# A hybrid decoder layer on one core: a recurrent head's last level computed from copies of its operands, right behind the level ahead of it

## The chip, the cores and the metric

The kernel runs on one core of a Trainium2 chip. It is written by hand for each engine: TensorE (PE) does matrix products into eight PSUM banks, VectorE (DVE) and ScalarE (ACT) do the elementwise work, GpSimd (POOL) sets up constants and SyncE (SP) issues the DMAs. The engines run side by side and meet only at semaphores that one raises and another waits for. The metric is the device time of one execution in microseconds (us), the median of several runs.

## What is computed

One decoder layer over 512 tokens of width 1024. A conditioned RMSNorm, one input projection, two groups of four heads each (a gated linear recurrence, HGRN2, and top-k sparse attention), one output projection, and a gated feed-forward part. The change touches the recurrent group only:

```python
def step(S, inp):
    qb, kb, vb, gb = inp            # gb: cumulated log of the forget gate f
    o_inter = einsum('bhtk,bhkv->bhtv', qb * exp(gb), S)
    diff = gb[:, :, :, None, :] - gb[:, :, None, :, :]
    decay = exp(where(causal[None, None, :, :, None], diff, -inf))
    A = einsum('bhtk,bhsk,bhtsk->bhts', qb, kb, decay)
    o_intra = einsum('bhts,bhsv->bhtv', A, vb)
    g_last = gb[:, :, -1]
    S_new = exp(g_last)[..., None] * S + einsum('bhsk,bhsv->bhkv', kb * exp(g_last - gb), vb)
    return S_new, o_inter + o_intra
```

So an output token t takes from each earlier token s the value v_s with weight q_t · k_s, and every channel of that product is shrunk by the product of the gates f between s and t.

## The kernel before

**Levels.** The kernel doesn't run the recurrence in time. For each head it builds the whole 512 x 512 triangle of weights in 10 levels (`LEVELS`, numbered 0 to 9). Level 0 is the diagonal. Level st from 1 pairs neighbouring blocks of `half` = 2^(st-1) tokens: keys of the left block with queries of the right one. The arrays `k_b` (keys) and `q_f` (queries), both 128 channels x 512 tokens, carry the product of gates inside their block. After each level st from 1 to 8, DVE widens the blocks in place: right halves of `q_f` times the total of the left block (L1105), left halves of `k_b` times the total of the right block (L1107), and the totals themselves pairwise (L1110, into `tot`). Since this is in place, DVE waits for PE's matmuls of the level (`lvl_mm`) first, and PE's next level waits for DVE (`lvl_ready`). Level 8 has two products of 128 x 128 (L1598), level 9 two of 128 x 256 (L1602): key blocks 0 and 1 against query blocks 2 and 3 together. Levels alternate between PSUM banks 2 and 3, which ACT (outer levels: L607, L608, L619, L624, L625, L627) and DVE (inner levels) empty.

**Filling.** Between two levels PE computes steps of the input projection of the next head, of four weight tiles f, q, i and g with 8 steps each. A step is three matmuls of 128 x 512 (L1342): the operands are split into a high and a low part. `LEVEL_STEPS` says how many of the 32 steps follow each level (31 of them; the last stands behind the output product of the head, L1629). In the last recurrent head the steps are those of the first attention head, 24 in place of 32, in the same proportion. Then follow one step, the sum of squares (L1637) and the next head.

**DVE's other work.** In the same levels DVE runs the top-k search of the attention (`LEVEL_ROUNDS`: 12 rounds for each head, a MAX8 at L1075 and a MATCH_REPLACE8 at L1080 each, over 256, 384 or 512 columns), and the low parts of weights (`split_lo`, L817). In the text of a level the order is: wait for `lvl_mm`, widen, MAX8s of its rounds, copy of an inner level, MATCH_REPLACE8s, `split_lo`. Rounds 7 and 8 stand in level 7, round 9 in level 8, rounds 10 and 11 in level 9. After level 9 come `hp` and `f_w` (L1083 to L1091), the start of the next head, or, after the last head, `att_rotate` (L1149 to L1154), for which PE waits at L1646. Heads 0 and 3 are written out for DVE, heads 1 and 2 are a loop; for PE heads 0 to 2 are a loop.

Of the kernel before, what the change touches and what calls it, by code (L numbers as in the profile page):

```python
# [30 lines left out]
P = 128  # L31
D_MODEL = 1024
SEQ = 512
# [24 lines left out]
IDX_COLS = IDX_HEADS * IDX_DIM + IK_COLS  # L58
IDX_ORDER = (4, 0, 1, 2, 3)
LEVELS = 10  # L60
LEVEL_STEPS = (0, 5, 3, 5, 2, 4, 4, 3, 3, 2)
LEVEL_ROUNDS = ((0,), (), (1, 2), (), (3, 4), (5,), (6,), (7, 8), (9,), (10, 11))
PARTNER_HEAD = [(r + 16) % 32 for r in range(32)]
ROUNDS = TOPK // 8
# [8 lines left out]
def build(nc, x, c, positions, w_ada, b_ada, norm_pre_mix, norm_post_mix, norm_pre_ffn, norm_post_ffn, w_in,  # L73
          hgrn_lower_bound, hgrn_out_norm, idx_k_norm_w, idx_k_norm_b, w_out, w_ffn_in, w_ffn_out, rope_const, out):
    f32, f32r, u32, i32 = mybir.dt.float32, mybir.dt.float32r, mybir.dt.uint32, mybir.dt.int32
    ALU, ACT = mybir.AluOpType, mybir.ActivationFunctionType
    ds = bass.ds
    ctx = ExitStack()
    with ctx:
# [12 lines left out]
        act = sb("act", FT * SEQ)  # L92
# [31 lines left out]
        def part(t, at, n=SEQ):  # L124
            return t[:, at:at + n]

        f_, q_silu = part(act, 0), part(act, 2 * SEQ)
        q_f, k_b, tot, i_t, i_tok, o_sq, o_rstd, o_n = (part(act, n * SEQ) for n in range(5, 13))
        att_hg = act[:, 13 * SEQ:13 * SEQ + 2560]  # L130
        at_diag = att_hg.rearrange("p (c x) -> p c x", x=SEQ + P)[:, :, 0:P]
# [72 lines left out]
        lvl_ready, lvl_mm, lvl_out, tot_ok = sem("lvl_ready"), sem("lvl_mm"), sem("lvl_out"), sem("tot_ok")  # L204
# [600 lines left out]
        def _(ve):  # L805
            V = nc.vector
# [7 lines left out]
            def split_lo(g, slot, n=1024):  # L814

                ve.wait_ge(hi_ok, g + 1)
                V.tensor_tensor(w_lo[slot][:, 0:n], w_raw[slot][:, 0:n], w_hi[slot][:, 0:n].bitcast(f32),  # L817
                                ALU.subtract).then_inc(lo_ok, 1)
# [250 lines left out]
            def hg_body(h):  # L1069
                def find_eight(n):  # L1070

                    t = n % 3 + 1
                    if not (isinstance(h, int) and h == 0 and n < 3):
                        wait_apart(top_rep, h * 12 + (n - 2))
                    V.max(top8[:, 8 * (t - 1):8 * t], sc_t[t]).then_inc(top_max, 1)  # L1075

                def take_eight(n):
                    t = n % 3 + 1
                    wait_apart(top_max, h * 12 + (n + 1))
                    V.match_replace(out=sc_t[t], in_to_replace=top8[:, 8 * (t - 1):8 * t], in_values=sc_t[t],  # L1080
                                    imm_value=TAKEN).then_inc(top_rep, 1)

                V.tensor_copy(hp[:, :], hg_par[:, ds(h * 3, 2)]).then_inc(hp_ok, 1)  # L1083
                ve.wait_ge(f_sig, h + 1)
                ve.wait_ge(hp_ok, 1 if isinstance(h, int) and h == 0 else h * 2)
                V.tensor_scalar(f_w, f_, hp[:, 0:1], hp[:, 1:2], ALU.mult, ALU.add).then_inc(f_ok, 1)
                ve.wait_ge(f_ok, h + 1)
                V.tensor_scalar(k_b, f_w, float(-HEAD ** -0.5), float(HEAD ** -0.5), ALU.mult,
                                ALU.add).then_inc(lvl_ready, 1)
                ve.wait_ge(q_ok, h + 1)  # L1090
                V.tensor_tensor(q_f, q_silu, f_w, ALU.mult).then_inc(lvl_ready, 1)  # L1091
                t_off = 0
                src = f_w
                for st in range(LEVELS):
                    half = 0 if st == 0 else 1 << (st - 1)
                    ve.wait_ge(lvl_mm, h * LEVELS + (st + 1))
                    if 0 < st < LEVELS - 1:

                        nb = SEQ // (2 * half)
                        qv = q_f.rearrange("p (b two h) -> p b two h", two=2, h=half)  # L1100
                        kv = k_b.rearrange("p (b two h) -> p b two h", two=2, h=half)
                        tv = src.rearrange("p (b two) -> p b two", two=2)
                        if st > 1:
                            ve.wait_ge(tot_ok, h * 8 + (st - 1))
                        V.tensor_tensor(qv[:, :, 1, :], qv[:, :, 1, :],  # L1105
                                        tv[:, :, 0:1].to_broadcast([P, nb, half]), ALU.mult)
                        V.tensor_tensor(kv[:, :, 0, :], kv[:, :, 0, :],  # L1107
                                        tv[:, :, 1:2].to_broadcast([P, nb, half]), ALU.mult).then_inc(lvl_ready, 1)
                        nxt = tot[:, t_off:t_off + nb]
                        V.tensor_tensor(nxt, tv[:, :, 0], tv[:, :, 1], ALU.mult).then_inc(tot_ok, 1)  # L1110
                        src, t_off = nxt, t_off + nb
                    rounds = LEVEL_ROUNDS[st]
                    for n in rounds:
                        find_eight(n)

                    pv = ps[2 + st % 2][:, 0:P].rearrange("p (c t) -> p c t", c=TT)
                    bv = blk.rearrange("p (c t) -> p c t", c=TT)
                    m = block_masks[:, None, min(st, 5) * 32:(min(st, 5) + 1) * 32]
                    if st == 0:
                        if not (isinstance(h, int) and h == 0):  # L1120
                            ve.wait_ge(blk_out, h)
                        V.tensor_tensor(bv, pv, m.to_broadcast([P, TT, 32]), ALU.mult).then_inc(lvl_out, 1)
                    elif st < 6:
                        wait_apart(lvl_out, h * 6 + st)
                        V.copy_predicated(bv, m.bitcast(u32).to_broadcast([P, TT, 32]), pv).then_inc(lvl_out, 1)
                    if st == 1:
                        if not (isinstance(h, int) and h == 0):
                            head_tail(h - 1)
                    for n in rounds:
                        take_eight(n)  # L1130
                    if isinstance(h, int) and h == HG_HEADS - 1:
                        if st in (1, 4, 9):
                            split_lo(*{1: (G_ATT + 1, 1), 4: (G_ATT + 2, 2), 9: (G_ATT + 3, 0)}[st])
                    elif st in (1, 3, 6, 8):
                        at, slot = {1: (5, 1), 3: (6, 2), 6: (7, 3), 8: (8, 0)}[st]
                        split_lo(h * 4 + (G_HG + at), slot)

            hg_body(0)
            with ve.Fori(1, HG_HEADS - 1) as h:
# [193 lines left out]
        def _(te):  # L1333
            mm = nc.tensor.matmul
# [83 lines left out]
            for t in range(TT):  # L1418
# [3 lines left out]
                for half in range(2):  # L1422
                    if t == 3 and half:
                        te.wait_ge(xt_high, 1)
                    for k in range(4):
                        at = t * D_MODEL + (4 * half + k) * P
                        last = nc.tensor.transpose(ps[2 * (t % 3) + half][:, k * P:(k + 1) * P], xn[:, at:at + P],
                                                   ident[:, :])
# [144 lines left out]
            def hg_body(h, last_head):  # L1573
                def level(st):
                    te.wait_ge(lvl_ready, h * LEVELS + (st + 1))
                    if st == 0:
                        te.wait_ge(q_ok, h + 1)

                    if 2 <= st < 8:
                        te.wait_ge(lvl_out, h * 6 + (st - 1))  # L1580
                    elif st >= 8:
                        te.wait_ge(outer_out, h * 4 + (st - 7))
                    bank = ps[2 + st % 2]
                    q = q_f if st else q_silu
                    if st < 7:
                        ahead = 32 if st == 6 else 0
                        for t in range(TT):
                            for j in (0, 2) if st == 6 else range(4):
                                at = t * P + 32 * j
                                last = mm(bank[32 * j:32 * j + 32, t * 32:(t + 1) * 32], k_b[:, at:at + 32],  # L1590
                                          q[:, at + ahead:at + ahead + 32], start=True, stop=True)
                    elif st == 7:
                        for t in range(TT):
                            last = mm(bank[0:64, t * 64:(t + 1) * 64], k_b[:, t * P:t * P + 64],
                                      q_f[:, t * P + 64:(t + 1) * P], start=True, stop=True)
                    elif st == 8:
                        for b in range(2):
                            last = mm(bank[:, b * P:(b + 1) * P], k_b[:, 2 * b * P:(2 * b + 1) * P],  # L1598
                                      q_f[:, (2 * b + 1) * P:(2 * b + 2) * P], start=True, stop=True)
                    else:  # L1600
                        for b in range(2):
                            last = mm(bank[:, b * 2 * P:(b + 1) * 2 * P], k_b[:, b * P:(b + 1) * P],  # L1602
                                      q_f[:, 2 * P:4 * P], start=True, stop=True)
                    last.then_inc(lvl_mm, 1)

                def project(n, count):
# [9 lines left out]
                for t in range(TT):  # L1616
                    last = nc.tensor.transpose(ps[6][:, t * P:(t + 1) * P], i_t[:, t * P:(t + 1) * P], ident[:, :])
# [91 lines left out]
            h = ATT_HEADS - 1  # L1709
# [142 lines left out]
```

## Time and profile before

| | us |
|---|---|
| median of 3 runs | 726.9 (726.54 to 729.52) |
| the profiled execution | 728.42 |
| its span in the trace | 726.7 |
| PE busy | 705.7 (97% of the span) |
| DVE busy | 434.0 (60%) |
| ACT busy | 296.2 (41%) |
| heads 0 to 3 of the recurrence, from 103.9 to 227.0 | 123.1 |

The profiled execution took 1.5 us more than the median, and 1.7 us of it lie outside the span of the instructions. A row of a timeline gives the start of an instruction and its length. The length of a matmul goes up to a modelled end, and the next one starts before that: what a matmul costs is read from the distance between starts. A floating-point matmul appears as two passes, so the two products of level 8 are a row of `x4`.

### The profile page before, as it was taken

The numbers are of one execution on the slowest core, as the hardware profiler recorded it, in microseconds if no ns is written. First come the engines' busy times: TensorE is split into PE (matmuls) and PEld (weight loads), VectorE is DVE, ScalarE is ACT, GpSimd is POOL, SyncE is SP. The second block draws the span as 40 slices with busy tenths as digits, with TensorE's granted clock in tenths as the row PEclk, the third lists the DMA queues.
The fourth block names the chain that finished last, engine by engine and source line by source line (L and its number), as shares of the span: only waits on it lengthen the run. The fifth ranks groups of instructions, "written<-read, shape, count | busy, mean of one in ns | idle before, by whom it ended". The sixth has DMA issues, their size and how long they took to land.

```text
span 726.7 us, 11020 instructions
## 1 busy us (share of the span) xinstructions
PE 705.7 (97%) x3962; PEld 552.7 (76%) x3962; DVE 434.0 (60%) x806; ACT 296.2 (41%) x472; POOL 11.1 (2%) x39
## 2 busy tenths in 40 slices
PE   5999999999999999999999999999999999999997
PEld 4565567777766878878888888888888788888885
DVE  3966678898898999968643433323432335443444
ACT  6445553535454444536572343342343332211223
POOL 4000000000000000000000000000000000000000
PEclk9999999999999999999899999999999999999999
DMA  9944023231222766567225532355533224223202
GB/s 314 358 144 114 3 59 85 62 116 53 62 60 87 217 217 223 182 209 205 81 59 145 144 105 78 106 144 144 144 94 108 87 87 132 99 87 102 71 0 117
DMA packets 95995, 89.10 MB, mean 123 GB/s; under 512 B 2950, under 2 KB 84954, under 8 KB 95964
## 3 DMA queue, kind: packets, MB, share of 16 engines
q1 hardware_dynamic: 95964, 88.70, 39.9%
q8 instruction: 18, 0.29, 0.2%
q14 instruction: 13, 0.11, 0.0%
HBM read 86.59 MB, written 2.10 MB: 122 GB/s over the span
## 4 chain that ended last, share of the span: by engine, by line
PE 61%; DVE 4%; issue 1%; ACT 0%; DVEq 0%; ACTq 0%
PE ps L1342 34%; PE ps L1363 17%; PE ps L1381 6%; DVE rope L892 1%; PE ps L1646 1%; PE ps L1402 1%; PE ps L1529 1%; DVE w_lo L817 1%; PE ps L1666 1%; PE ps L1778 1%; PE ps L1782 1%; PE ps L1779 1%; PE ps L1523 0%; DVE act L1149 0%; DVE res L1154 0%
## 5 line engine op out<-in xcount | busy, mean ns | idle before, releaser
L1342 PE MATMUL ps<-h_hi,w_hi 128*128 128x512 f32 x560 | 227.3, 406 | 0.0
L1342 PE MATMUL ps<-h_hi,w_lo 128*128 128x512 f32 x560 | 218.7, 391 | 0.0
L1342 PE MATMUL ps<-h_lo,w_hi 128*128 128x512 f32 x560 | 218.3, 390 | 0.0
L817 DVE TENSOR_TENSOR w_lo<-w_raw,w_hi 128x1024 fp32r<-128x1024 f32 (+1 forms) x109 | 129.3, 1187 | 99.4 <-ACT w_hi L462 98.9
L462 ACT ACTIVATE w_hi<-w_raw 128x1024 fp32r<-128x1024 f32 (+1 forms) x109 | 111.6, 1029 | 105.9 <-PE ps L1363 86.3
L1342 PEld LDWEIGHTS ps<-h_hi,w_hi 128*128 128x128 f32 x560 | 105.2, 188 | 30.3 <-issue 9.1
L1342 PEld LDWEIGHTS ps<-h_hi,w_lo 128*128 128x128 f32 x560 | 105.1, 188 | 22.6
L1342 PEld LDWEIGHTS ps<-h_lo,w_hi 128*128 128x128 f32 x560 | 105.3, 188 | 20.7 <-issue 1.0
L1363 PE MATMUL ps<-w_hi,h_hi 128*128 128x512 f32 x176 | 70.1, 398 | 0.8 <-DVE mix L1214 0.8
L1363 PE MATMUL ps<-w_hi,h_lo 128*128 128x512 f32 x176 | 68.6, 390 | 0.0
L1363 PE MATMUL ps<-w_lo,h_hi 128*128 128x512 f32 x176 | 68.5, 389 | 0.0
L794 ACT ACTIVATE adaw<-ps 128x512 f32<-128x512 f32 x22 | 13.2, 598 | 132.0 <-PE ps L1342 130.2
L1272 DVE TENSOR_TENSOR act<-adaw,ps 128x512 f32 (+1 forms) x22 | 15.1, 687 | 57.2 <-PE ps L1342 57.2
L1295 DVE CAST h_hi<-act 128x512 fp32r (+1 forms) x22 | 9.4, 426 | 56.8 <-PE ps L1363 53.7
L1363 PEld LDWEIGHTS ps<-w_hi,h_hi 128*128 128x128 f32 x176 | 33.0, 188 | 8.3 <-DVE mix L1214 1.0
L1363 PEld LDWEIGHTS ps<-w_lo,h_hi 128*128 128x128 f32 x176 | 33.1, 188 | 7.2 <-issue 0.5
L1363 PEld LDWEIGHTS ps<-w_hi,h_lo 128*128 128x128 f32 x176 | 33.0, 188 | 6.9
L1075 DVE MAX8 top<-score 128x8 f32<-128x256 f32 (+2 forms) x48 | 25.2, 552 | 6.1 <-PE ps L1590 5.8
L1080 DVE MATCH_REPLACE8 score<-top,score 128x256 f32<-128x256 f32 (+2 forms) x48 | 25.8, 543 | 0.0
L1381 PE MATMUL ps<-w_hi,h_hi 128*128 128x512 f32 x64 | 24.9, 389 | 0.0
L1381 PE MATMUL ps<-w_lo,h_hi 128*128 128x512 f32 x64 | 24.9, 389 | 0.0
L1381 PE MATMUL ps<-w_hi,h_lo 128*128 128x512 f32 x64 | 24.9, 389 | 0.0
(250 smaller groups left out, 791.9 us busy)
## 6 DMA issues: line engine op xcount, KB each, us to landing
w_raw<-in_w_ffn_in SPq DMA_DIRECT2D x44, 512.0 KB, 5.7
w_raw<-in_w_in SPq DMA_DIRECT2D x28, 512.0 KB, 3.8
w_raw<-in_w_ffn_out SPq DMA_DIRECT2D x22, 512.0 KB, 3.5
adaw<-in_w_ada SPq DMA_DIRECT2D x12, 512.0 KB, 3.9
act<-in_w_ada SPq DMA_DIRECT2D x12, 512.0 KB, 9.2
adaw<-in_w_ada SPq DMA_DIRECT2D x6, 1024.0 KB, 5.3
act<-in_w_ada SPq DMA_DIRECT2D x6, 1024.0 KB, 5.1
res<-in_x SPq DMA_DIRECT2D x8, 512.0 KB, 4.7
```

Of the source, the lines that this page charges most:

```text
L462: sc.activation(w_hi[slot][:, 0:n], w_raw[slot][:, 0:n], ACT.Copy).then_inc(hi_ok, 1)
L794: sc.activation(silu_g[u // 2], ps[u][:, :], ACT.Silu).then_inc(silu_done[u // 2], 1)
L817: V.tensor_tensor(w_lo[slot][:, 0:n], w_raw[slot][:, 0:n], w_hi[slot][:, 0:n].bitcast(f32), ALU.subtract).then_inc(lo_ok, 1)
L892: V.scalar_tensor_tensor(out=total, in0=w, scalar=silu, in1=total, op0=ALU.mult, op1=ALU.add).then_inc(sum_used, 1)
L1075: V.max(top8[:, 8 * (t - 1):8 * t], sc_t[t]).then_inc(top_max, 1)
L1080: V.match_replace(out=sc_t[t], in_to_replace=top8[:, 8 * (t - 1):8 * t], in_values=sc_t[t], imm_value=TAKEN).then_inc(top_rep, 1)
L1272: V.tensor_tensor(act[:, ds(i * 2 * SEQ + v * SEQ, SEQ)], silu_g[v], ps[2 * v + 1][:, :], ALU.mult).then_inc(act_ok[v], 1)
L1295: V.tensor_copy(h_hi[:, at], act[:, ds(k * SEQ, SEQ)]).then_inc(xs_hi, 1)
L1342: last = mm(ps[bank][0:rows, :], a, b, start=(k == 0 and n == 0), stop=(k == KT - 1 and n == 2))
L1363: last = mm(ps[2 * t + b][:, :], a, w, start=(first and n == 0), stop=(last_one and n == 2))
L1381: last = mm(ps[2 * t + b][:, :], a, w, start=False, stop=(n == 3 and m == 2))
L1402: return nc.tensor.transpose(ps[k][:, t * P:(t + 1) * P], xn[:, t * D_MODEL + k * P:t * D_MODEL + (k + 1) * P], ident[:, :])
```

## The change

1. `LEVEL_STEPS` goes from `..., 4, 4, 3, 3, 2` to `..., 4, 4, 4, 0, 4` for levels 5 to 9: four steps ahead of level 8, none between levels 8 and 9, four behind.
2. `q_last` and `k_last`, 128 columns each, are new places in a part of `act` that nothing else uses at that time.
3. In level 8 DVE no longer widens in place. It writes `q_last` from query block 3 and `k_last` from key block 0, with no wait for PE's level 8; the third operation, the totals, is left out. `tot_ok` so counts 7 for each head.
4. In level 9 DVE doesn't wait for PE before rounds 10 and 11. That wait now stands at the end of the head.
5. PE's level 9 is four products of 128 x 128 in place of two of 128 x 256: `k_last` and key block 1, each against query block 2 and `q_last`.

```diff
-LEVEL_STEPS = (0, 5, 3, 5, 2, 4, 4, 3, 3, 2)
+LEVEL_STEPS = (0, 5, 3, 5, 2, 4, 4, 4, 0, 4)
...
+        k_last, q_last = part(act, SEQ, P), part(act, SEQ + P, P)
...
-                    ve.wait_ge(lvl_mm, h * LEVELS + (st + 1))
-                    if 0 < st < LEVELS - 1:
+                    if st < 8:
+                        ve.wait_ge(lvl_mm, h * LEVELS + (st + 1))
+                    if st == 8:
+                        ve.wait_ge(tot_ok, h * 7 + 7)
+                        V.tensor_scalar(q_last, q_f[:, 3 * P:4 * P], src[:, 2:3], None, ALU.mult)
+                        V.tensor_scalar(k_last, k_b[:, 0:P], src[:, 1:2], None, ALU.mult).then_inc(lvl_ready, 1)
+                    elif 0 < st < 8:
...
+                ve.wait_ge(lvl_mm, h * LEVELS + LEVELS)
...
-                        for b in range(2):
-                            last = mm(bank[:, b * 2 * P:(b + 1) * 2 * P], k_b[:, b * P:(b + 1) * P],
-                                      q_f[:, 2 * P:4 * P], start=True, stop=True)
+                        for b, k_block in enumerate((k_last, k_b[:, P:2 * P])):
+                            for t, q_block in enumerate((q_f[:, 2 * P:3 * P], q_last)):
+                                last = mm(bank[:, (2 * b + t) * P:(2 * b + t + 1) * P], k_block, q_block, start=True,
+                                          stop=True)
```

PE, the last recurrent head, from level 8 (L1598) on, before:

```order
L1598 MATMUL ps<-act 128x128 [waits outer_out,lvl_ready]
L1598 MATMUL ps<-act 128x128
L1342 MATMUL ps<-h_hi,w_hi 128x512
L1342 MATMUL ps<-h_lo,w_hi 128x512
L1342 MATMUL ps<-h_hi,w_lo 128x512
L1342 MATMUL ps<-h_hi,w_hi 128x512
L1342 MATMUL ps<-h_lo,w_hi 128x512
L1342 MATMUL ps<-h_hi,w_lo 128x512
L1602 MATMUL ps<-act 128x256 [waits outer_out,lvl_ready]
L1602 MATMUL ps<-act 128x256
```

and in the changed kernel, where the same lines are 8 or 9 further down (a step is L1350, level 8 is L1606, level 9 is L1611), from the last step ahead of level 8:

```order
L1350 MATMUL ps<-h_hi,w_hi 128x512
L1350 MATMUL ps<-h_lo,w_hi 128x512
L1350 MATMUL ps<-h_hi,w_lo 128x512
L1606 MATMUL ps<-act 128x128 [waits outer_out,lvl_ready]
L1606 MATMUL ps<-act 128x128
L1611 MATMUL ps<-act 128x128 [waits outer_out,lvl_ready]
L1611 MATMUL ps<-act 128x128 x3
```

The two steps that stood between the levels are gone from there: one stands ahead of level 8, the other behind level 9. In heads 0 to 2 three steps stood there; one is ahead of level 8 and two are behind level 9.

DVE, the looped head, from the MAX8s of rounds 7 and 8 to round 9, before:

```order
L1075 MAX top<-score 128x8 [waits top_rep] x2
L810 REGISTER_ALU
L1080 MATCH_REPLACE score<-top,score 128x384 [waits top_max]
L810 REGISTER_ALU
L1080 MATCH_REPLACE score<-top,score 128x512 [waits top_max]
L1096 REGISTER_ALU
L1104 REGISTER_ALU [waits lvl_mm]
L1105 TENSOR_TENSOR act<-act 128x2x128 [waits tot_ok]
L1107 TENSOR_TENSOR act<-act 128x2x128
L1110 TENSOR_TENSOR act<-act 128x2
L1075 MAX top<-score 128x8 [waits top_rep]
```

and in the changed kernel:

```order
L1076 MAX top<-score 128x8 [waits top_rep] x2
L811 REGISTER_ALU
L1081 MATCH_REPLACE score<-top,score 128x384 [waits top_max]
L811 REGISTER_ALU
L1081 MATCH_REPLACE score<-top,score 128x512 [waits top_max]
L1100 REGISTER_ALU
L1101 TENSOR_SCALAR act<-act 128x128 [waits tot_ok]
L1102 TENSOR_SCALAR act<-act 128x128
L1076 MAX top<-score 128x8 [waits top_rep]
```

The operations that make level 9's operands keep their place behind the four top-k operations of rounds 7 and 8. They are two of 128 columns in place of three, and the wait for PE ahead of them is gone.

## Rows read from the trace of the kernel before

**Rows 1.** Stretch table, head 1: length, busy time of each engine (instructions).
```profile
135.50:167.20 31.70, 31.70 (x337) 23.65 (x336) 27.85 (x77) 15.70 (x26) 0.00 (x0) 1.00 0.27 83
```

**Rows 2.** Waits of PE: total us, times, longest us.
```profile
PE ps L1590 <- DVE act L1107: 1.3, 3, 0.6
...
PE ps L1602 <- DVE act L1107: 0.4, 1, 0.4
PE ps L1646 <- DVE res L1154: 0.3, 1, 0.3
```

**Rows 3.** Timeline of PE around levels 8 and 9 of head 1: start, length.
```profile
158.15 0.39 PE L1342 MATMUL ps<-h_hi,w_lo 128*128 128x512 f32 x1
158.38 0.60 PE L1598 MATMUL ps<-act 128*128 128x128 f32 x4
...
159.05 0.40 PE L1342 MATMUL ps<-h_lo,w_hi 128*128 128x512 f32 x1
...
160.65 0.39 PE L1342 MATMUL ps<-h_hi,w_lo 128*128 128x512 f32 x1
160.88 1.02 PE L1602 MATMUL ps<-act 128*128 128x256 f32 x4
...
161.97 0.40 PE L1342 MATMUL ps<-h_lo,w_hi 128*128 128x512 f32 x1
```

**Rows 4.** Timeline of DVE, the same stretch of head 1.
```profile
158.80 0.68 DVE L1080 MATCH_REPLACE8 score<-top,score 128x512 f32<-128x512 f32 x1
159.39 0.42 DVE L1105 TENSOR_TENSOR act<-act 128x256 f32<-128x256 f32 x1
```

**Rows 5.** Timelines: DVE's scaling of 128 columns by a column, and the next operation.
```profile
233.72 0.29 DVE L1166 TENSOR_SCALAR res<-res,ri 128x128 f32<-128x128 f32 x1
233.93 1.22 DVE L817 TENSOR_TENSOR w_lo<-w_raw,w_hi 128x1024 fp32r<-128x1024 f32 x1
```

**Rows 6.** Timeline of PE in the last head, levels 8 and 9.
```profile
218.44 0.61 PE L1598 MATMUL ps<-act 128*128 128x128 f32 x4
...
220.05 0.40 PE L1342 MATMUL ps<-h_hi,w_lo 128*128 128x512 f32 x1
220.85 1.13 PE L1602 MATMUL ps<-act 128*128 128x256 f32 x4 [0.41 <-DVE act L1107]
...
222.05 0.40 PE L1342 MATMUL ps<-h_lo,w_hi 128*128 128x512 f32 x1
```

**Rows 7.** Timeline of DVE in the last head, levels 8 and 9.
```profile
220.05 0.41 DVE L1105 TENSOR_TENSOR act<-act 128x256 f32<-128x256 f32 x1
220.39 0.41 DVE L1107 TENSOR_TENSOR act<-act 128x256 f32<-128x256 f32 x1
...
220.79 0.41 DVE L1075 MAX8 top<-score 128x8 f32<-128x256 f32 x1
...
222.16 1.15 DVE L1075 MAX8 top<-score 128x8 f32<-128x384 f32 x2 [0.32 <-PE ps L1602]
```

**Rows 8.** Timelines of heads 0 and 2: PE's level 8, DVE's widening after it.
```profile
126.74 0.60 PE L1598 MATMUL ps<-act 128*128 128x128 f32 x4
...
127.66 0.42 DVE L1105 TENSOR_TENSOR act<-act 128x256 f32<-128x256 f32 x1
...
190.01 0.60 PE L1598 MATMUL ps<-act 128*128 128x128 f32 x4
...
191.03 0.42 DVE L1105 TENSOR_TENSOR act<-act 128x256 f32<-128x256 f32 x1
```

**Rows 9.** Timeline of ACT, head 1: the copy out of level 7's bank.
```profile
158.80 0.36 ACT L619 ACTIVATE act<-ps 64x256 f32<-64x256 f32 x1
```

**Rows 10.** Timelines: the end of DVE's rotation and PE's first attention logits.
```profile
230.38 0.68 DVE L1154 TENSOR_TENSOR res<-act 32x512 f32<-32x512 f32 x1
...
230.38 0.39 PE L1342 MATMUL ps<-h_hi,w_lo 128*128 128x512 f32 x1
231.12 0.92 PE L1646 MATMUL ps<-res 128*128 128x128 f32 x4 [0.35 <-DVE res L1154]
```

**Rows 11.** Groups by form: DVE's smallest multiplication, and its wait at a head's start.
```profile
L1075 DVE MAX8 top<-score 128x8 f32<-128x256 f32 x16 | 6.8, 424 | 5.8 <-PE ps L1590 5.8
...
L1110 DVE TENSOR_TENSOR act<-act 128x2 f32<-128x2 f32 x4 | 0.6, 156 | 0.0
```

**Rows 12.** The weight loads of level 9 over all four heads, each in ns.
```profile
L1602 PEld LDWEIGHTS ps<-act x16: 186/188/190, 129.0 to 221.4; 128*128 128x128 f32 x16
```

More of the change, by code:

```diff
@@ L1103, in hg_body @@
                         if st > 1:
-                            ve.wait_ge(tot_ok, h * 8 + (st - 1))
+                            ve.wait_ge(tot_ok, h * 7 + (st - 1))
                         V.tensor_tensor(qv[:, :, 1, :], qv[:, :, 1, :],
```

## The prediction, as it stood before the changed kernel ran

> **What bounds the kernel now.** I start with the table by stretches. In head 1 of the recurrence PE is busy for all of its 31.70 us, DVE for 27.85 and ACT for 15.70 [rows 1]. So a stage's time is the sum of PE's starts, and an edit pays only if it takes away matmul time or a wait of PE. The list of PE's waits comes next. Behind DVE's widening (L1107) PE stands 1.3 us ahead of levels of 32 tokens, 0.4 us ahead of level 9, and it stands 0.3 us ahead of the attention logits [rows 2]. All of these are in or right behind the last recurrent head; heads 0 to 2 have none at levels 8 and 9. Then the timelines of PE and DVE side by side, since the question is whether DVE delivers level 9's operands in time once the steps between the levels are gone.
>
> From the timeline of PE I read what levels cost. One matmul of a step takes 0.23 us, start to start. From the last matmul ahead of level 8 to the second behind it are 0.90 us (158.15 to 159.05); less two matmuls, 0.46, level 8 costs 0.44. The same for level 9: 160.65 to 161.97 is 1.32, less 0.46 is 0.86 [rows 3]. Both have four passes and four weight loads, level 9 twice the columns and twice the time. So the time follows the columns, 0.11 us for a pass of 128, and loads and the change between forms cost about nothing. There is hardly anything to win by standing back to back.
>
> **Steps moved (part 1).** PE has the same number of steps in every head: 31 and one, or 24 in the last. Nothing is gained by moving them alone. In heads 0 to 2, one step of three matmuls, 0.69 us, goes ahead of level 8, and level 9 comes right behind it, 0.43 us after level 8's start. Without any wait level 9 of head 1 would start at 158.38 + 0.69 + 0.43 = 159.50.
>
> **Level 9's operands (parts 2 and 3).** DVE makes them behind four top-k operations of rounds 7 and 8. In head 1 the last of these starts at 158.80, and the next operation starts at 159.39 [rows 4]. It did not wait for PE there, so to take away its wait for level 8 doesn't bring it forward. The new operation, a scaling of 128 columns by a column, has a near relative: L1166 takes 0.29 us, and the next operation starts 0.21 us behind it [rows 5]. So the second one ends at 159.39 + 0.21 + 0.29 = 159.89. PE took 0.05 us from the end of L1107 (220.39 + 0.41 = 220.80) to its start at 220.85 [rows 6, 7], which gives 159.94. That is 0.44 us later than PE would be there. A PE that has stood also shows its first weight load: behind the wait in the last head, level 9 took 1.20 us to the second matmul of the step (220.85 to 222.05) where head 1 took 1.09 (160.88 to 161.97), 0.11 more [rows 3, 6]. Head 1 loses **0.55 us**, a wait that isn't there now.
>
> Head 0: level 9 without a wait at 126.74 + 1.12 = 127.86, operands at 127.66 + 0.55 = 128.21, so 0.35 + 0.11 = **0.46**. Head 2: 190.01 + 1.12 = 191.13 against 191.03 + 0.55 = 191.58, so 0.45 + 0.11 = **0.56** [rows 8]. Nothing behind swallows this: the wait of DVE for PE at a head's start (5.8 us in four heads, rows 11) shows that DVE follows PE there, so that what PE loses stays lost. What is queued behind PE's new wait are level 9, the steps of the next projection and the output product; ACT's copy of level 9 waits for it, with four steps of cover.
>
> In the last head only two steps stood between the levels, and PE waits at level 9 already. Now: 220.28 would have been its start (220.05 + 0.23), 220.85 it was, so 0.57 + 0.11 = 0.68 lost [rows 6]. Then: level 9 without a wait at 218.44 + 1.12 = 219.56; the operands at 220.05 + 0.55 = 220.60 [rows 7]; lost 1.04 + 0.11 = 1.15. **0.47 more.**
>
> Bounds for the new operations: not less than the smallest multiplication, 0.156 us [rows 11], with the next starting some 0.07 behind it, so 0.28 in place of 0.55 until PE starts; not more than L1107 in the form of now, 0.41 us, next start at 0.34 [rows 7], so 0.80. Over four heads this is 1.1 us less or 1.0 more. I take L1166: same operation, same form.
>
> At 128 columns L1166 (0.29) costs what I would give a product of two tensors of that size. The Trainium skill, VectorE: DVE Perf Modes, section "Walkthrough: the 8-slice pipeline in each mode", says that a scaling by a scalar reads one tensor through both ports and does two results a cycle even in fp32, a product of two tensors only one. The row already has whatever comes of that, so the sum stays; were it read as half of L1107's 0.34 spacing, 0.17, level 9 would come about 0.04 us earlier in each head.
>
> **DVE's wait at level 9 (part 4).** DVE loses no time in the last head between the widening and rounds 10 and 11. Level 8's part falls from 0.74 us (220.05 to 220.79) to 0.42, and the wait of 0.32 ahead of the MAX8 at 222.16 goes [rows 7]: DVE is 0.64 earlier. The rotation follows it directly, so its end, 230.38 + 0.68 = 231.06, moves to 230.42. PE would be there at 230.38 + 0.23 = 230.61, 0.47 later by the loss above: 231.08. So PE's wait at L1646 goes, 231.12 - 230.61 = 0.51 and the shown load, 0.12: **0.63 us won** [rows 10]. In heads 0 to 2 an earlier DVE only waits longer for PE's level 0.
>
> **Four products in place of two (part 5).** Same columns, eight passes of 0.11 in place of four of 0.21, so 0.88 against 0.86: nothing, or 0.02 us a head. The four loads more lie under passes, as in level 8.
>
> The bank of level 7 is what level 9 writes: ACT's copy ends at 158.80 + 0.36 = 159.16 [rows 9], 0.34 us ahead of 159.50. It isn't late as long as DVE is later, and it would be the next to bind if DVE were faster.
>
> **The sum:** 0.46 + 0.55 + 0.56 + 0.47 - 0.63 = +1.4 us. On the profiled execution that is 728.42 + 1.4 = 729.8; its 1.5 us above the median has nothing to do with the change, so the median goes from 726.9 to **728.3 us**. By the bounds of the new operations: +0.3 to +2.4, 727.2 to 729.3.
>
> **Rivals.**
> 1. *Faster: DVE isn't late.* Level 9's operands lie ready in every head. Then both waits of the last head are gone, 0.68 + 0.63, and the median is 725.6. For it: the wait for PE's level 8 is gone and the work is smaller. Against: the MATCH_REPLACE8 in front ends after level 8's start by 0.9 to 1.0 us in heads 0 to 2, and DVE did not wait at that place [rows 3, 4, 8]. It decides if the operands are ready 0.4 us earlier than I have them.
> 2. *Slower than before by more: the loads show.* Four weight loads more in each head, of 0.188 us [rows 12]. If back-to-back passes of 128 columns can't cover them, 4 x 4 x 0.188 = 3.0 us on top of 1.4: 731.3. Against: level 8, where three of four loads follow a pass of 128 columns, costs 0.44, half of level 9 [rows 3]. It decides from the point where a load takes longer than the 0.11 us of a pass. The Trainium skill, TensorE: Matmul & The Clock Gate, section "LDWEIGHTS (loading the stationary operand)", gives columns divided by 1.2 in ns, 107 ns for 128 columns. By that estimate the load just fits under a pass of 0.11, and fully shown it would be 16 x 0.107 = 1.7 us, not 3.0. Level 8's row agrees that it is covered.
> 3. *No difference.* PE's new waits are swallowed later, at waits PE has anyway, and the median stays at 726.9. Against: the engines it would wait for follow PE in every head [rows 11].
>
> **How the numbers follow.** The forecast gets 0.72, rival 1 0.10, rival 2 0.07, rival 3 0.11. The range has to hold the forecast's 727.2 to 729.3, rival 3, and some tenths of spread between medians of three (the lower two of the runs of before lie 0.4 apart, the third 2.6 higher): 725.9 to 730.2. A measurement of this kernel tells 0.5%, 3.6 us, from no change. Rival 2 alone passes it, and only just with its full price; no case reaches 723.3. So faster 0.02, same 0.92, slower 0.06. Within that my sign is slower.
>
> **What the profile after would show.** PE's waits: a line of level 9 (now L1611) behind DVE's scaling (L1102), four times, 0.2 to 0.4 us in heads 0 to 2 by the profile's count and 0.9 in the last; no line of the logits behind the rotation. Right of part 5: from level 8's start to the second step matmul behind level 9 1.5 us where no wait stands between. DVE's scaling at about 0.29 us. I would be wrong if level 9 starts 0.43 us behind level 8 in the looped heads (rival 1), or if its eight passes take clearly more than 0.9 us (rival 2), or if the stretch from one head's level 0 to the next is still 31.6 us in heads 0 and 1 (rival 3).

## The result, and the profile after

The changed kernel is slower by a fifth of a percent. Over 22 runs of each kernel its median is 729.2 us against 727.88 before; the ratio is 1.0019, with a 95% interval of 1.0010 to 1.0028, so 0.7 to 2.0 us. One run of the kernel before took 3988 us and is not in the ratio; without it the median is the same to 0.02 us. The forecast was +1.4 us on a median of 726.9, which came from three runs; over 22 it is 727.88. So the change is as forecast, and the time itself is 0.9 us above the forecast's 728.3.

The profiled executions differ by less: the span is 727.5 us after and 726.7 before. So the heads are measured inside the trace, between marks that every kernel has: the start of level 0 in each head, the first attention logits, and the matmul of the output projection (L1363, now L1371) that waits for the last attention head's output (DVE, L1214, now L1222), which is the end of the attention. Earlier matmuls of that line fill gaps of the attention. Before and after:

```profile
316.45 0.50 PE L1363 MATMUL ps<-w_hi,h_hi 128*128 128x512 f32 x1 [0.78 <-DVE mix L1214]
```

```profile
319.21 0.50 PE L1371 MATMUL ps<-w_hi,h_hi 128*128 128x512 f32 x1 [0.78 <-DVE mix L1222]
```

All numbers below are distances between such starts.

| us | head 0 | head 1 | head 2 | head 3, to the logits | level 0 to logits | to the end of the attention |
|---|---|---|---|---|---|---|
| before | 31.64 | 31.64 | 31.63 | 32.30 | 127.21 | 212.54 |
| changed | 32.17 | 32.26 | 32.25 | 32.23 | 128.91 | 214.13 |
| difference | +0.53 | +0.62 | +0.62 | -0.07 | +1.70 | +1.59 |

PE's waits in the changed kernel, over the whole run, in the form of [rows 2] (who, for whom, total us, times, longest):

```profile
PE ps L1611 <- DVE act L1102: 1.7, 4, 0.8
PE ps L1598 <- DVE act L1113: 1.3, 3, 0.6
```

Level 9 (L1611) now waits in all four heads for DVE's second scaling (L1102). Before it waited once, for 0.4. The three waits ahead of small levels are the same 1.3 us. The line of the first logits behind the rotation is gone. Head by head the profile gives level 9 a wait of 0.25, 0.34, 0.33 and 0.83.

Head 1, PE, from the last matmul of a step ahead of level 8 to the second one behind level 9; it answers to [rows 3]:

```profile
160.52 0.39 PE L1350 MATMUL ps<-h_hi,w_lo 128*128 128x512 f32 x1
160.75 0.60 PE L1606 MATMUL ps<-act 128*128 128x128 f32 x4
161.69 1.15 PE L1611 MATMUL ps<-act 128*128 128x128 f32 x8 [0.34 <-DVE act L1102]
162.60 0.47 PE L1350 MATMUL ps<-h_hi,w_hi 128*128 128x512 f32 x1
162.91 0.39 PE L1350 MATMUL ps<-h_lo,w_hi 128*128 128x512 f32 x1
```

and DVE beside it, which answers to [rows 4]:

```profile
160.49 0.68 DVE L1081 MATCH_REPLACE8 score<-top,score 128x512 f32<-128x512 f32 x1
161.08 0.28 DVE L1101 TENSOR_SCALAR act<-act 128x128 f32<-128x128 f32 x1
161.28 0.28 DVE L1102 TENSOR_SCALAR act<-act 128x128 f32<-128x128 f32 x1
```

Level 8 starts at 160.75, so level 9 was due at 161.18. DVE began its first scaling at 161.08, right behind the last top-k operation and with no wait ahead of it. It ended the second at 161.56, and level 9 started at 161.69: 0.51 late.

The last head, PE, which answers to [rows 6] and [rows 10]:

```profile
222.07 0.61 PE L1606 MATMUL ps<-act 128*128 128x128 f32 x4
...
223.51 1.16 PE L1611 MATMUL ps<-act 128*128 128x128 f32 x8 [0.83 <-DVE act L1102]
...
224.74 0.39 PE L1350 MATMUL ps<-h_lo,w_hi 128*128 128x512 f32 x1
...
233.76 0.39 PE L1350 MATMUL ps<-h_hi,w_lo 128*128 128x512 f32 x1
233.99 0.82 PE L1655 MATMUL ps<-res 128*128 128x128 f32 x4
```

Level 9 comes 1.44 us behind level 8 in place of 0.43. The first logits come 0.23 behind the matmul ahead of them, which is no wait at all; before it was 0.74.

### The profile page after: what moved, and what is told of

It reads as the page before. It is cut to its first block, busy times and chain, and to the rows that moved or that the text cites. A ratio compares the mean times of both kernels' runs of the same rounds, so it can differ in the third digit from the quotient of the medians.

```text
span 727.5 us, 11044 instructions
## 1 busy us (share of the span) xinstructions
PE 704.7 (97%) x3978; PEld 551.7 (76%) x3978; DVE 432.5 (59%) x802; ACT 296.5 (41%) x472; POOL 11.1 (2%) x39
## 4 chain that ended last, share of the span: by engine, by line
PE 64%; DVE 2%; issue 0%; DVEq 0%; ACT 0%
PE ps L1350 35%; PE ps L1371 17%; PE ps L1389 6%; PE ps L1675 1%; PE ps L1655 1%; PE ps L1410 1%; PE ps L1787 1%; PE ps L1788 1%; PE ps L1791 1%; PE ps L1537 0%; PE ps L1531 0%; PE ps L1668 0%; DVE w_lo L818 0%; DVE act L1157 0%; DVE act L893 0%
## 5 line engine op out<-in xcount | busy, mean ns | idle before, releaser
L1350 PE MATMUL ps<-h_hi,w_hi 128*128 128x512 f32 x560 | 226.6, 405 | 0.0
L1350 PE MATMUL ps<-h_hi,w_lo 128*128 128x512 f32 x560 | 218.7, 391 | 0.0
L1350 PE MATMUL ps<-h_lo,w_hi 128*128 128x512 f32 x560 | 218.3, 390 | 0.0
L1350 PEld LDWEIGHTS ps<-h_hi,w_hi 128*128 128x128 f32 x560 | 105.1, 188 | 30.3 <-issue 9.1
L1350 PEld LDWEIGHTS ps<-h_hi,w_lo 128*128 128x128 f32 x560 | 105.1, 188 | 22.6
L1350 PEld LDWEIGHTS ps<-h_lo,w_hi 128*128 128x128 f32 x560 | 105.3, 188 | 20.9 <-issue 1.0
L1371 PE MATMUL ps<-w_hi,h_hi 128*128 128x512 f32 x176 | 70.1, 398 | 0.8 <-DVE mix L1222 0.8
L1371 PE MATMUL ps<-w_hi,h_lo 128*128 128x512 f32 x176 | 68.6, 390 | 0.0
L1371 PE MATMUL ps<-w_lo,h_hi 128*128 128x512 f32 x176 | 68.5, 389 | 0.0
L1371 PEld LDWEIGHTS ps<-w_hi,h_hi 128*128 128x128 f32 x176 | 33.0, 188 | 8.3 <-DVE mix L1222 1.0
L1371 PEld LDWEIGHTS ps<-w_lo,h_hi 128*128 128x128 f32 x176 | 33.1, 188 | 7.1 <-issue 0.5
L1371 PEld LDWEIGHTS ps<-w_hi,h_lo 128*128 128x128 f32 x176 | 33.0, 188 | 7.0
L1076 DVE MAX8 top<-score 128x8 f32<-128x256 f32 (+2 forms) x48 | 25.1, 552 | 8.7 <-PE ps L1598 8.7
```

The lines of the kernel that those rows point to most:

```text
L1350: last = mm(ps[bank][0:rows, :], a, b, start=(k == 0 and n == 0), stop=(k == KT - 1 and n == 2))
L1371: last = mm(ps[2 * t + b][:, :], a, w, start=(first and n == 0), stop=(last_one and n == 2))
```

## The experiments

Theory W is the prediction's: PE's matmul time is what it was, and the loss is PE waiting at level 9 for operands that DVE makes behind top-k rounds 7 and 8. Rival L says that eight passes of 128 columns with eight weight loads cost more than four of 256. Rival M says that moving steps is free and places of their own don't matter, rival B that standing back to back saves time in itself. e2, e3 and e7 ran ten to twelve times; the others ran once and are judged by their marks. Their single times are 726.12 (e1), 728.48 (e4), 725.49 (e5), 730.35 (e6) and 727.35 (e8).

| us | head 0 | head 1 | head 2 | head 3, to the logits | level 0 to logits | to the end of the attention |
|---|---|---|---|---|---|---|
| before | 31.64 | 31.64 | 31.63 | 32.30 | 127.21 | 212.54 |
| changed | 32.17 | 32.26 | 32.25 | 32.23 | 128.91 | 214.13 |
| e1, own places, old steps | 31.66 | 31.65 | 31.64 | 31.51 | 126.46 | 211.81 |
| e2, operands first | 31.65 | 31.63 | 31.63 | 31.65 | 126.56 | 211.91 |
| e3, steps alone | 32.81 | 32.90 | 32.90 | 32.46 | 131.07 | 216.31 |
| e4, five and three steps | 31.63 | 31.64 | 31.64 | 31.53 | 126.44 | 211.77 |
| e5, operands first, old steps | 31.64 | 31.64 | 31.66 | 31.63 | 126.57 | 211.87 |
| e6, two more operations | 32.53 | 32.64 | 32.66 | 32.62 | 130.45 | 215.71 |
| e7, rounds behind the rotation | 31.65 | 31.63 | 31.64 | 31.08 | 126.00 | 211.24 |
| e8, PE's heads written out | 32.12 | 32.18 | 32.18 | 32.21 | 128.69 | 213.95 |

**e1: own places, the steps of before.**

```diff
-LEVEL_STEPS = (0, 5, 3, 5, 2, 4, 4, 4, 0, 4)
+LEVEL_STEPS = (0, 5, 3, 5, 2, 4, 4, 3, 3, 2)
```

> The changed kernel with the projection steps of before (3 ahead of level 8, 3 between, 2 behind), so that only the operands in places of their own and the moved waits are left. Theory W (PE's loss is the wait of level 9 for operands that DVE makes behind the top-k rounds 7 and 8): three steps lie between the levels again, so no wait in heads 0 to 2, 31.64 us from level 0 to level 0 as before (32.2 in the changed kernel). Last head: level 9 waits 0.43 in place of 0.68, and the wait at the first attention logits all but goes. From the first level 0 to the first logits 126.6 us (before 127.2, changed kernel 128.9). Rival L (eight passes of 128 columns with their eight weight loads are what costs): heads 0 to 2 stay at 32.2, 128.2 us to the logits.

Measured: 31.64 to 31.66 us a head, 126.46 to the logits. The whole loss is gone with the old steps, although level 9 still has its eight passes. Rival L falls. It also shows that places of their own, with the waits and the totals that go with them, are worth 0.75 us by themselves, all of it in the last head. DVE there ends the rotation 31.45 us after level 0, where before it was 32.24 (198.82 to 231.06). Level 9 of that head still waits for DVE; PE then comes to the logits just as the rotation ends, at 230.38:

```profile
229.70 0.68 DVE L1162 TENSOR_TENSOR res<-act 32x512 f32<-32x512 f32 x1
```

```profile
230.44 0.92 PE L1655 MATMUL ps<-res 128*128 128x128 f32 x4
```

**e2: the operands ahead of the top-k rounds.** In level 7, behind the totals, and no longer in level 8:

```diff
                         src, t_off = nxt, t_off + nb
+                    if st == 7:
+                        ve.wait_ge(tot_ok, h * 7 + 7)
+                        V.tensor_scalar(q_last, q_f[:, 3 * P:4 * P], src[:, 2:3], None, ALU.mult)
+                        V.tensor_scalar(k_last, k_b[:, 0:P], src[:, 1:2], None, ALU.mult).then_inc(lvl_ready, 1)
```

> The changed kernel with its steps (4, 0, 4), but DVE makes q_last and k_last directly behind the widening after level 7, ahead of rounds 7 and 8. Theory W: the operands are ready about 1.5 us ahead of level 9, which then starts 0.43 to 0.45 us behind level 8 in all heads; heads 0 to 2 back at 31.64 us. In the last head the wait at level 9 goes, but DVE's rotation ends when it did in the changed kernel against the head's start, so PE meets it at the logits: 126.7 us from the first level 0 to the first logits, 0.5 under before. Rival L: level 9 starts without a wait but its passes take 0.5 us longer, heads stay at 32.2. Whole time: W says 0.5 us under before, 2.2 under the changed kernel.

Measured: as W had it, 31.63 to 31.65 a head and 126.56 to the logits; over ten runs a ratio of 0.9985 to before (0.9972 to 0.9998), 1.1 us less; the medians lie 0.7 apart. Head 1, DVE and then PE:

```profile
158.15 0.16 DVE L1112 TENSOR_TENSOR act<-act 128x4 f32<-128x4 f32 x1
158.35 0.29 DVE L1116 TENSOR_SCALAR act<-act 128x128 f32<-128x128 f32 x1
158.55 0.28 DVE L1117 TENSOR_SCALAR act<-act 128x128 f32<-128x128 f32 x1
158.75 1.15 DVE L1076 MAX8 top<-score 128x8 f32<-128x384 f32 x2
```

```profile
159.91 0.39 PE L1350 MATMUL ps<-h_hi,w_lo 128*128 128x512 f32 x1
160.13 0.60 PE L1606 MATMUL ps<-act 128*128 128x128 f32 x4
160.58 1.06 PE L1611 MATMUL ps<-act 128*128 128x128 f32 x8
...
161.70 0.40 PE L1350 MATMUL ps<-h_lo,w_hi 128*128 128x512 f32 x1
```

The operands are ready at 158.83, 1.75 us ahead of level 9, which starts 0.45 behind level 8. From 159.91 to 161.70 are 1.79; less two matmuls, 0.46, levels 8 and 9 cost 1.33. Before they cost 0.44 + 0.86 = 1.30. So the eight passes cost 0.03 us more than the four, as good as nothing. In the last head, PE no longer waits at level 9, and meets DVE at the logits instead:

```profile
230.82 0.68 DVE L1162 TENSOR_TENSOR res<-act 32x512 f32<-32x512 f32 x1
```

```profile
231.55 0.92 PE L1655 MATMUL ps<-res 128*128 128x128 f32 x4 [0.35 <-DVE res L1162]
```

The rotation ends at 231.50 and the logits start at 231.55. DVE is what bounds the last head from here on. The new place has a price there. The first scaling stands right behind the totals and waits for them: it starts 0.20 behind them (158.15 to 158.35), where before the next operation came after 0.07 (157.08 to 157.15). The rotation ends 31.60 us after the head's level 0, in e1 after 31.45, and e1 is 0.10 ahead to the logits. The rows fit that wait as the cause; no run takes it away alone.

**e3: the steps alone, on the kernel before.**

```diff
-LEVEL_STEPS = (0, 5, 3, 5, 2, 4, 4, 3, 3, 2)
+LEVEL_STEPS = (0, 5, 3, 5, 2, 4, 4, 4, 0, 4)
```

> The kernel before with only the steps moved (4, 0, 4): level 9's operands are still widened in place, after level 8. Theory W: DVE may start only when level 8 is through, and level 9 waits for two operations of 128x256: 1.16 us lost in each of heads 0 to 2 (1.24 if a release takes 0.13 there), 0.7 more than before at level 9 of the last head, less the 0.63 at the logits. 32.8 to 32.9 us a head, 131.0 us from the first level 0 to the first logits, whole time 3.7 us over before. Rival M (moving the steps is free, places of their own don't matter): like before.

Measured: 32.81 to 32.90 a head, 131.07 to the logits, and over ten runs 1.0049 (1.0034 to 1.0065), 3.6 us more. In head 1 level 8 starts at 160.91 and level 9 at

```profile
162.53 1.13 PE L1602 MATMUL ps<-act 128*128 128x256 f32 x4 [1.02 <-DVE act L1107]
```

Rival M falls: what the move costs depends on what DVE has to do between the levels. The move costs 3.9 us by the marks, and places of their own take 2.2 of them back (131.07 to 128.91), but not all.

**e4: five steps ahead, three behind.**

```diff
-LEVEL_STEPS = (0, 5, 3, 5, 2, 4, 4, 4, 0, 4)
+LEVEL_STEPS = (0, 5, 3, 5, 2, 4, 4, 5, 0, 3)
```

> The changed kernel with five steps ahead of level 8, none between, three behind; DVE's order untouched. Theory W: one step more, 0.69 us, covers the 0.51 us by which the operands are late in heads 0 to 2: no wait there, 31.64 us a head, level 9 0.43 us behind level 8. Last head: level 9 waits about 0.4. 126.6 us from the first level 0 to the first logits. Rival L: level 9 behind level 8 costs 0.5 us whatever stands ahead, heads stay at 32.2.

Measured: 31.63 to 31.64 a head, 126.44 to the logits. One step more ahead of level 8 covers the lateness in heads 0 to 2, with DVE's order untouched. In the last head level 9 still comes 0.77 behind level 8 (220.72 to 221.49), and as in e1 that is hidden at the logits. So this kernel, with the changed kernel's operations and back-to-back levels, is at e1's time, and 0.12 ahead of e2. The wait is DVE's distance to PE and nothing that belongs to levels 8 and 9.

**e5: operands first, the steps of before.** e2's edit, with e1's line of steps.

> Operands made directly behind level 7's widening, and the steps of before (3, 3, 2). Against the same with the steps (4, 0, 4) this tells what standing back to back is worth when nobody waits. Theory W and the rows of before (a level costs its columns, the change between forms 0.01 us): nothing, 31.64 us a head and 126.7 us to the first logits, within 0.1. Rival B (back to back saves time): 31.7 or more a head.

Measured: 126.57 to the logits against 126.56 in e2. In both DVE's rotation bounds the last head (PE waits 0.34 and 0.35 at the logits), so the heads before it must tell: heads 0 to 2 take 94.94 us together in e5 and 94.91 in e2. Where nobody waits, to stand back to back is worth 0.01 us a head. Rival B falls, and with it any gain the new order could have had on PE.

**e6: two more operations ahead of the operands.**

```diff
                         ve.wait_ge(tot_ok, h * 7 + 7)
+                        for at in (SEQ + 2 * P, SEQ + 3 * P):
+                            V.tensor_scalar(part(act, at, P), q_f[:, 3 * P:4 * P], src[:, 2:3], None, ALU.mult)
                         V.tensor_scalar(q_last, q_f[:, 3 * P:4 * P], src[:, 2:3], None, ALU.mult)
```

> The changed kernel with two more scalings of 128 columns on DVE ahead of q_last and k_last in each head (into places nobody reads). Theory W: each puts the operands 0.2 us later, and PE follows one for one: level 9 starts 0.4 us later, 32.6 us a head in heads 0 to 2, and the last head loses 0.4 too; 130.5 us from the first level 0 to the first logits. If PE's wait were a fixed cost of the release and not DVE's lateness: 128.9 as in the changed kernel.

Measured: 0.36, 0.38, 0.41 and 0.39 us more a head than the changed kernel, 130.45 to the logits. DVE's starts are 0.2 apart, two of them 0.4. What DVE is late, PE loses one for one.

**e7: operands first, and the last head's rounds 10 and 11 behind the first rotation.** e2's edit, and

```diff
-                    rounds = LEVEL_ROUNDS[st]
+                    rounds = () if st == 9 and isinstance(h, int) and h == HG_HEADS - 1 else LEVEL_ROUNDS[st]
...
                     att_rotate(0)
+                    for n in LEVEL_ROUNDS[9]:
+                        t = n % 3 + 1
+                        ve.wait_ge(top_rep, (HG_HEADS - 1) * 12 + (n - 2))
+                        V.max(top8[:, 8 * (t - 1):8 * t], sc_t[t]).then_inc(top_max, 1)
+                    for n in LEVEL_ROUNDS[9]:
+                        t = n % 3 + 1
+                        ve.wait_ge(top_max, (HG_HEADS - 1) * 12 + (n + 1))
+                        V.match_replace(out=sc_t[t], in_to_replace=top8[:, 8 * (t - 1):8 * t], in_values=sc_t[t],
+                                        imm_value=TAKEN).then_inc(top_rep, 1)
                     ve.wait_ge(top_rep, HG_HEADS * 12)
```

> Operands directly behind level 7's widening, steps (4, 0, 4), and in the last head rounds 10 and 11 of the top-k search behind the first rotation of the attention. Theory W: neither level 9 nor the first logits wait any more, 125.9 us from the first level 0 to the first logits, 1.3 under before. The rounds then run beside the logits, where DVE has waited for PE. If DVE is late there instead, the gain is lost at the softmax of the first attention head. Whole time 1.3 us under before (0.2%), 2.7 under the changed kernel.

Measured: 126.00 to the logits and 211.24 to the end of the attention, 1.21 and 1.30 under before, so nothing of it is lost in the attention. The rotation and the moved rounds, on DVE, and PE's first logits:

```profile
227.69 0.68 DVE L1162 TENSOR_TENSOR res<-act 32x512 f32<-32x512 f32 x1
228.30 1.14 DVE L1171 MAX8 top<-score 128x8 f32<-128x384 f32 x2
...
230.69 0.29 DVE L1193 CUSTOM_DVE_ANT_0 res<-ps,bias 128x128 f32<-128x128 f32 x1
```

```profile
230.14 0.81 PE L1664 MATMUL ps<-res 128*128 128x128 f32 x4
```

The rounds lie where DVE would have stood for PE's logits. Over twelve runs the median is 726.3 us against 727.4 before, ratio 0.9986 (0.9974 to 0.9999): by the marks the fastest of all. Of the versions that ran more than once, e2 and e7 are ahead of before. They can't be told apart by their runs (by the ratios 1.1 and 1.0 us under before), only by the marks, where e7 is 0.67 ahead.

**e8: PE's heads 0 to 2 written out.**

```diff
-            with te.Fori(0, HG_HEADS - 1) as h:
+            for h in range(HG_HEADS - 1):
                 hg_body(h, False)
```

> The changed kernel with PE's heads 0 to 2 written out in place of a loop; DVE and ACT untouched. It asks why each of heads 0 to 2 lost 0.07 us more than forecast: in the changed kernel level 9 starts 0.13 us after the end of DVE's second scaling in these heads and 0.05 in the last, which is the only one that PE has outside a loop. Theory R (in the loop the wait compares with a register and stands on an instruction of its own, ahead of the matmul): 0.05 in all four heads, level 9 starts 0.08 earlier in heads 0 to 2, some 32.1 to 32.2 us a head at most. Rival (it is DVE's side, or the neighbours on PE): 0.13 stays in heads 0 to 2.

Measured, DVE and PE in head 1:

```profile
160.87 0.28 DVE L1102 TENSOR_SCALAR act<-act 128x128 f32<-128x128 f32 x1
```

```profile
161.21 1.16 PE L1611 MATMUL ps<-act 128*128 128x128 f32 x8 [0.26 <-DVE act L1102]
```

From the end at 161.15 to the start at 161.21 are 0.06 us; in the changed kernel it was 0.13 (161.56 to 161.69). It is 0.06 in heads 0 and 2 as well, and the heads take 32.12, 32.18 and 32.18. So in this loop a wait that ends late costs 0.07 us more; e3 and e6 have the same 0.13 in heads 0 to 2 and 0.05 to 0.06 in the last. e8 changes these things together and doesn't tell which of them costs the 0.07. The Trainium skill, Advanced Engine Details and Errata, section "Network/Comms", lists 50 to 100 ns for a sequencer's read of a semaphore's value; the 0.07 measured here is of that size, though no run here shows that this read is the cause.

## Why the prediction was right

- **PE's own time.** "Hardly anything to win by standing back to back", and the price of eight passes at 0 to 0.02 us: e5 against e2 gives 0.01, e2's levels 8 and 9 0.03 more than before. Right.
- **Level 9's wait in heads 0 to 2.** Forecast 0.46, 0.55 and 0.56, measured 0.53, 0.62 and 0.62. The mechanism was right (e1, e2, e4 and e6), the size 0.07, 0.07 and 0.06 low. The term that was too small was PE's answer to DVE: 0.05 us, read in the last head [rows 6, 7], was used for heads in a loop, where it is 0.13. e8 shows the difference. The scaling itself was read well: 0.28 us in place of 0.29, next start after 0.20 in place of 0.21. The 0.17 that the prediction weighed, half of L1107's 0.34, did not come. The forms of L1166 in the trace of before show why:

```profile
L1166 DVE TENSOR_SCALAR res<-res,ri 128x512 f32<-128x512 f32 x4 | 1.9, 486 | 0.1
L1166 DVE TENSOR_SCALAR res<-res,ri 128x128 f32<-128x128 f32 x4 | 1.1, 287 | 0.1
```

  From 128 to 512 columns the mean grows by 199 ns, which is 66 ns for each 128. So 0.22 of the 0.29 us don't shrink with the columns, and a halved spacing leaves that out.
- **The last head.** Forecast 0.47 more at level 9 and 0.63 won at the logits, of which 0.12 shows only behind their start; no row is given for it. So -0.04 to the logits; measured -0.07. From the first logits to the row behind them it was 0.76 before (231.12 to 231.88) and is 0.65 now (233.99 to 234.64), so that part is 0.11. Right. DVE's rotation came 0.78 earlier against the head's start, not 0.64; PE was later still, so it changed nothing.
- **The sum.** +1.4 forecast; the marks give +1.59 to the end of the attention. The difference is the 0.20 of heads 0 to 2, less the 0.03 and plus the 0.01 of the last. The runs give +1.4 (0.7 to 2.0). That their value falls on the forecast itself is luck: by the marks the sum was 0.2 low, which this interval can't show. So is the median of three that the forecast starts from, 1.0 below that of 22 runs.
- **Rival 1.** It gave 725.6 if DVE were early in every head, two waits of the last head gone. e2 makes that case, and shows the price was wrong: only 0.65 us to the logits and 0.63 to the end of the attention, not 1.3, because PE without the wait at level 9 arrives at the logits before DVE's rotation ends. The prediction's own numbers had it: PE at 230.61 - 0.68 = 229.93, the rotation at 230.42. The rival counted both waits as if they were independent; the second is what the first had been covering. Only e7, which also moves work out of DVE's way, gets 1.30. (The "0.9 to 1.0" in its argument is when the operation behind the MATCH_REPLACE8 starts; by its row in [rows 4] this ends 1.10 behind level 8. It makes no difference here.)
- **Rival 2** fell with e1 and e2; **rival 3** with the marks: +1.70 to the logits is still +1.59 at the end of the attention. DVE followed PE at the heads' starts: its wait there (now L1076 for L1598) grew from 5.8 to 8.7 us in four heads.
- **The bank of level 7**, named as next to bind: in e2 ACT's copy in head 1 (L620) ends at 159.87 + 0.36 = 160.23, 0.35 us ahead of level 9's start at 160.58, so it didn't bind; the forecast had 0.34.

## What to carry to other kernels

Work that stands between two dependent steps of the busy engine is cover for the engine that prepares the second; before it is moved, the preparer's queue has to be read up to the operation that releases, not only the operation's own length. A wait for the other engine that is taken away helps only if the operation waited there. In heads 0 to 2 it stood in a queue behind four others, and the cure was its place in that queue (e2) or one step more of cover (e4). The new order of steps gave nothing by itself: with the old one, places of their own are as fast (e1). Two waits in a row on the same chain are not a sum; the second may be as long as it is only because the first has been paid.

## What was not expected of the hardware

**The clock around the sums.** The span grew by 0.8 us where the heads alone lost 1.6. The rest lies outside the change. Level 0 of head 0 began 1.17 us later (105.08 against 103.91), and the stretch from the 32 matmuls of one column that sum the conditioning (L1529, now L1537) to the first matmul of the feed-forward part was 1.96 us shorter. Three kernels, the two rows of PE that fill this stretch, before, after and e5:

```profile
349.23 4.83 PE L1529 MATMUL ps<-ones,rope 128*128 128x1 f32 x32
353.92 5.79 PE L1402 MATMUL ps<-ident,act 128*128 128x128 f32 x32
```

```profile
352.00 3.63 PE L1537 MATMUL ps<-ones,rope 128*128 128x1 f32 x32
355.48 5.36 PE L1410 MATMUL ps<-ident,act 128*128 128x128 f32 x32
```

```profile
349.65 3.63 PE L1537 MATMUL ps<-ones,rope 128*128 128x1 f32 x32
353.14 3.69 PE L1410 MATMUL ps<-ident,act 128*128 128x128 f32 x32
```

and the stretch tables for pieces of it, whose third number from the end is the granted clock as a share of 2.4 GHz, again before, after and e5:

```profile
353.00:357.00 4.00, 4.00 (x20) 4.00 (x21) 2.10 (x5) 0.84 (x4) 0.00 (x0) 0.50 0.40 117
```

```profile
356.00:361.00 5.00, 4.84 (x30) 4.60 (x27) 3.25 (x7) 1.89 (x7) 0.00 (x0) 0.66 0.37 105
```

```profile
349.00:358.00 9.00, 8.41 (x71) 7.87 (x69) 7.00 (x13) 6.51 (x17) 0.00 (x0) 1.00 0.21 61
```

Before, the clock fell to the lower level, 1.2 GHz, in the midst of the sums; in the changed kernel it was low only in part of the transposes; in e5 it stayed at 2.4 GHz. What the engine did ahead of a fall were these sums, matmuls of one column, behind dense work at full clock. The same work took 11.1, 9.1 and 7.8 us, and 9.4 in e1 and 11.0 in e4. So this piece, which nobody touched, moves the time of one execution by up to 3.3 us, twice the effect under study, and single runs of e1 (726.12), e4 (728.48) and e5 (725.49) say little. It isn't a matter of the version: among 17 runs of before, the six with a mean granted clock of 0.997 or 0.998 took 725.2 to 726.2 us, the two with 0.991 took 728.6 and 728.8. Only marks inside the trace, or many runs, measure an edit of this size here.
